# The down projection of a decoder block as seven Strassen products instead of one full product

## What the kernel must compute

```python
h = modulate(rms_norm(x, norm_ffn_g), sh2, sc2)          # 1024 x 1024
gu = silu(h @ w_gate) * (h @ w_up)                       # 1024 x 2816
x = x + g2 * (gu @ w_down)                               # w_down is 2816 x 1024
return rms_norm(x, final_norm_g)
```

## Time and profile before

| | |
|---|---|
| median of three runs | 1543.34 us (1543.19 to 1545.88) |
| the profiled execution, its own time | 1546.7 us |
| its span, first to last instruction | 1545.0 us |
| mean granted TensorE clock | 0.977 |
| PE busy | 1441.9 us, 93% of the span |
| DVE, ACT, POOL busy | 54%, 45%, 44% |
| gate and up products on PE | from 854 us to 1289.5 us |
| down products on PE | from 1289.5 us to 1537.9 us |

### The profile page before, as it was taken

One profiled execution on the slowest core, in us unless ns is written; L12 is line 12 of the kernel. 1 busy time (PEld: TensorE's weight loads), 2 busy tenths in 40 slices (PEclk: granted clock), 3 DMA queues, 4 the chain that ended last, 5 costly groups with the idle time before them and its releaser, 6 DMA issues.

```text
span 1545.0 us, 20466 instructions
## 1 busy us (share of the span) xinstructions
PE 1441.9 (93%) x7471; PEld 1225.5 (79%) x7471; DVE 831.4 (54%) x1479; ACT 694.1 (45%) x1334; POOL 676.0 (44%) x464
## 2 busy tenths in 40 slices
PE   1899899999999989899899899999999999899998
PEld 1887688887889978889688678888888887788886
DVE  5645879994644656654545763443333333615414
ACT  4524446631656655666633544333333331423321
POOL 2331222161110422062000898888888882642640
PEclk9999999999999998999799999999999999999999
DMA  9121122331203442210411032222222226653641
GB/s 372 46 82 57 66 83 81 133 129 62 77 29 124 138 163 88 92 62 21 151 55 42 31 106 82 83 82 82 82 82 82 82 96 229 215 156 138 204 135 55
DMA packets 106541, 161.27 MB, mean 104 GB/s; under 512 B 7021, under 2 KB 65573, under 8 KB 105418
## 3 DMA queue, kind: packets, MB, share of 16 engines
q1 hardware_dynamic: 106442, 159.97, 30.8%
HBM read 127.37 MB, written 32.58 MB: 104 GB/s over the span
## 4 chain that ended last, share of the span: by engine, by line
PE 82%; DVE 8%; issue 3%; ACT 3%; DMA 3%; POOL 1%; SPq 1%; DVEq 0%; ACTq 0%; POOLq 0%
PE PS L1775 21%; PE PS L1776 21%; PE PS L1777 21%; PE PS L1943 6%; PE PS L1913 5%; PE PS L1930 2%; PE PS L1931 2%; DMA rawb<-in_w_down_dram 1%; DVE LP L1504 1%; PE PS L1929 1%; DVE acc L1207 1%; PE PS L1975 1%; DVE marks_c L1344 1%; DMA adar<-in_ada_w_dram 1%; DVE sel L1311 1%
## 5 line engine op out<-in xcount | busy, mean ns | idle before, releaser
L839 POOL TENSOR_TENSOR BS<-rawb,BS 128x1024 fp32r<-128x1024 f32 x44 | 107.3, 2443 | 127.6 <-ACT BS L1123 127.6
L826 POOL TENSOR_TENSOR WS<-WSf,WS 128x512 fp32r<-128x512 f32 x110 | 162.7, 1487 | 0.7 <-ACT WS L1067 0.7
L1067 ACT CAST WS<-WSf 128x512 fp32r<-128x512 f32 x110 | 68.4, 622 | 202.1 <-POOL WSf L816 201.1
L816 POOL TENSOR_TENSOR WSf<-rawg 128x512 f32<-128x512 f32 x55 | 77.3, 1406 | 172.0 <-PE PS L1777 170.8
L1943 PE MATMUL PS<-Vn,PT 128*128 128x64 f32 x1152 | 145.4, 273 | 0.0
L1775 PE MATMUL PS<-BS,AS 128*128 128x512 f32 x352 | 137.9, 392 | 6.9 <-POOL BS L839 6.6
L1943 PEld LDWEIGHTS PS<-Vn,PT 128*128 128x128 f32 x1152 | 141.8, 195 | 0.0
L1775 PE MATMUL PS<-yh,WS 128*128 128x512 f32 x352 | 137.9, 392 | 2.9 <-DVE yl L1636 2.9
L1777 PE MATMUL PS<-yh,WS 128*128 128x512 f32 x352 | 137.7, 391 | 0.0
L1776 PE MATMUL PS<-yl,WS 128*128 128x512 f32 x352 | 137.5, 391 | 0.0
L1777 PE MATMUL PS<-BS,AS 128*128 128x512 f32 x352 | 137.4, 390 | 0.0
(11 more groups left out here) (300 smaller groups left out, 3530.7 us busy)
## 6 DMA issues: line engine op xcount, KB each, us to landing
rawb<-in_w_down_dram SPq DMA_DIRECT2D x44, 512.0 KB, 3.5
adar<-in_ada_w_dram SPq DMA_DIRECT2D x32, 512.0 KB, 3.8
raw<-in_w_in_dram SPq DMA_DIRECT2D x24, 512.0 KB, 3.9
qkv_scratch<-stage SPq DMA_DIRECT2D x48, 256.0 KB, 2.0
rawg<-in_w_gate_dram SPq DMA_DIRECT2D x22, 512.0 KB, 4.7
rawu<-in_w_up_dram SPq DMA_DIRECT2D x22, 512.0 KB, 4.3
gu_scratch<-Cu SPq DMA_DIRECT2D x44, 256.0 KB, 2.0
rawa<-gu_scratch SPq DMA_DIRECT2D x44, 256.0 KB, 3.5
```

The lines of the kernel that those rows point to most:

```text
L816: pool.tensor_tensor(WSf[m % N_SLOT][:], left(i, mat, a), left(i, mat, b), ALU.add if sign > 0 else ALU.subtract).then_inc(ws_sum, 1)
L826: pool.tensor_tensor(lo, WSf[m % N_SLOT][:] if b else left(i, mat, a), hi.bitcast(F32), ALU.subtract).then_inc(ws_ready, 1)
L839: pool.tensor_tensor(b[:, 1, :], rawb[m % 2][:], b[:, 0, :].bitcast(F32), ALU.subtract).then_inc(gb_lo, 1)
L1067: act.copy(WS[m % N_SLOT][:, 0], src).then_inc(ws_hi, 1)
```

## The change

The down projection becomes seven products of half matrices. gu is split into quadrants by odd and even hidden block and by token half, w_down by odd and even hidden block and by column half. For each of the seven forms, in the order of `DOWN`, 11 steps are run, one for each pair of hidden blocks, so 77 steps in place of 44. A step loads one 128x512 block of a gu quadrant or of a sum of two, and one or two 128x512 blocks of w_down, and runs 12 matmuls into four PSUM banks; consecutive products use the two halves of PSUM in turn.

- In the gate and up stage DVE forms five sums or differences of gu quadrants in each round (`gu_sum`) and SP stores them. With "22" and "11", which are stored as they are, seven blocks are stored in a round where there were four.
- In the down stage POOL forms the sum or difference of two w_down blocks for five of seven products (`down_sum`, 55 steps), and the `lo` part for the steps that are not in `DOWN_BY_V`. These 20 steps (four in each of those five products) get the `lo` part of the weights from DVE.
- `rawa` has three buffers, `rawb` four (each of two 128x512 parts). AS and BS keep six slots.
- Finished products are copied by ACT (form 1 into two quadrants, forms 5 and 4 into one) or added and subtracted by DVE (`down_evac`) in four held quadrants CD; the last use of a quadrant goes through g2 and the residual. They stand in DVE's program behind every second `down_low`.
- The eight residual loads are issued one by one, behind steps 11, 13, ... 25, g2 behind step 28 and the gain behind step 44. Step 4's loads stand with those of steps 0 to 3, ahead of the last stores.
- The last four tiles: GpSimd multiplies their left half by the gain ahead of time, ACT squares that half ahead of time and scales it at the end, DVE does the right half.

The diff, cut to its core:

```diff
+DOWN = ["1", "5", "3", "4", "2", "7", "6"]
+N_DOWN = len(DOWN) * PAIRS
+DOWN_SLOTS = 6
+DOWN_RAW_A = 3
+DOWN_RAW_B = 4
+GU_SUM = {"2": ("12", "22", 1), "7": ("21", "22", -1), "1": ("11", "22", 1), "5": ("11", "21", 1), "6": ("12", "11", -1)}
+RIGHT = {"1": ((0, 0), (1, 1), 1), "2": ((0, 0), None, 0), "3": ((0, 1), (1, 1), -1), "4": ((1, 0), (0, 0), -1),
+         "5": ((1, 1), None, 0), "6": ((0, 0), (0, 1), 1), "7": ((1, 0), (1, 1), 1)}
+DOWN_BY_V = [m for m in DOWN_SUMS if m % PAIRS % 3 == 1]
...
@@ SP
             def load_down(m):
+                form, j = DOWN[m // PAIRS], m % PAIRS
+                if m >= DOWN_RAW_A:
+                    sp.wait_ge(ga_lo, m - DOWN_RAW_A + 1)
...
+                sp.wait_ge(gu_out[form], GU_BASE[form] + 16 * (j + 1))
+                sp.dma_start(rawa[m % DOWN_RAW_A][:], gu_dram[int(form) - 1, j]).then_inc(ga_in[m % DOWN_RAW_A], 16)
+                if m >= DOWN_RAW_B:
+                    low_done(sp, m - DOWN_RAW_B)
+                elif m % 2 == 0:
+                    sp.wait_ge(ws_ready, AT_FF[PAIRS - 1, m // 2, FORMS[-1]] + 1)
+                for e, part in enumerate(RIGHT[form][0:2]):
+                    if part:
+                        row, col = (2 * j + part[0]) * P, part[1] * BANK
+                        sp.dma_start(rawb[m % DOWN_RAW_B][:, e, :],
+                                     w_down[row:row + P, col:col + BANK]).then_inc(gb_in[m % DOWN_RAW_B], 16)
...
+            for m in range(5, N_DOWN):
+                load_down(m)
+                if m == 7:
+                    store_sums(PAIRS - 1)
+                step, rest = divmod(m - PAIRS, 2)
+                if rest == 0 and 0 <= step < TT:
+                    sp.wait_ge(x_tile[step], 48)
+                    sp.dma_start(x1s[step // 4][:, step % 4, :], x1_dram[step * P:(step + 1) * P, :]).then_inc(x1_in, 16)
@@ POOL
+            for m in range(N_DOWN):
+                if m + 1 in DOWN_SUMS:
+                    down_sum(m + 1)
+                if m not in DOWN_BY_V:
+                    down_part(m)
@@ ACT
             def down_high(m):
+                before = m - DOWN_SLOTS
                 if m < 2:
                     act.wait_ge(x_lo, 3)
+                elif before < 0:
                     act.wait_ge(pr_pe, len(SEQ_FF))
+                elif before % PAIRS == PAIRS - 1:
+                    act.wait_ge(dn_pe, TT // 2 * (before // PAIRS + 1))
                 else:
+                    act.wait_ge(dj_pe, before - before // PAIRS + 1)
...
+                if m in DOWN_SUMS:
+                    act.wait_ge(gb_sum, DOWN_SUMS.index(m) + 1)
+                act.copy(BS[m % DOWN_SLOTS][:, 0, :], rawb[m % DOWN_RAW_B][:, 0, :]).then_inc(gb_hi, 1)
@@ DVE
             def down_low(m):
...
+                if m in DOWN_BY_V:
+                    b = BS[m % DOWN_SLOTS]
+                    dve.wait_ge(gb_hi, m + 1)
+                    dve.tensor_tensor(b[:, 1, :], rawb[m % DOWN_RAW_B][:, 0, :], b[:, 0, :].bitcast(F32),
+                                      ALU.subtract).then_inc(gb_lo_v, 1)
 
             for m, (i, mat, form) in enumerate(SEQ_FF):
                 combine(m)
+                if mat == 0 and i >= 1 and form in ("2", "4", "3"):
+                    gu_sum(i - 1, 2 + ("2", "4", "3").index(form))
...
                 if mat == 1 and form == "7":
                     gate_times_up(i, "22", 3, 7)
                     gate_times_up(i, "11", 4, 8)
+                    gu_sum(i, 0)
+                    gu_sum(i, 1)
...
+            def down_result(q, p, tt, held=True):
+                half, col = int(q[0]) - 1, int(q[1]) - 1
+                cols = slice(col * BANK, (col + 1) * BANK)
+                ps = PS[:, 4 * (p % 2) + tt, :]
+                if held:
+                    chained(dve.tensor_tensor(ps, ps, CD[q][:, tt, :], ALU.add))
+                chained(dve.tensor_tensor(ps, ps, g2r[:, cols], ALU.mult))
+                return dve.tensor_tensor(x1s[half][:, tt, cols], ps, x1s[half][:, tt, cols], ALU.add)
...
+                if form == "5":
+                    last = down_add("11", p, tt, ALU.subtract)
+                elif form == "3":
+                    chained(down_add("22", p, tt, ALU.add))
+                    last = down_result("12", p, tt)
+                elif form == "4":
+                    last = down_add("11", p, tt, ALU.add)
+                elif form == "2":
+                    chained(down_add("22", p, tt, ALU.subtract))
+                    chained(down_result("21", p, tt))
+                    ps = PS[:, 4 * (p % 2) + tt, :]
+                    chained(dve.tensor_tensor(ps, CD["22"][:, tt, :], g2r[:, BANK:D], ALU.mult))
+                    last = dve.tensor_tensor(x1s[1][:, tt, BANK:D], ps, x1s[1][:, tt, BANK:D], ALU.add)
+                elif form == "7":
+                    last = down_result("11", p, tt)
+                else:
+                    last = down_result("22", p, tt, held=False)
...
+            for m in range(2, N_DOWN + 2 * TT):
+                if m < N_DOWN:
+                    down_low(m)
+                if m < len(GU_ORDER):
+                    gu_sum(PAIRS - 1, m)
+                p, j = divmod(m - PAIRS - DOWN_SLOTS, PAIRS)
+                if p >= 1 and p < len(DOWN) - 1 and j % 2 == 0 and j < TT:
+                    down_evac(p, j // 2)
@@ PE
+            for p in range(len(DOWN)):
+                late = LATE_DOWN if p == len(DOWN) - 1 else 1
+                for j in range(PAIRS - late):
+                    m = p * PAIRS + j
                     pe.wait_ge(ga_lo, m + 1)
+                    low_done(pe, m)
                     for tt in range(TT // 2):
+                        if j == 0:
+                            bank_free(p, tt)
+                        last = down(m, tt, j == 0, False)
                     last.then_inc(dj_pe, 1)
```

More of the change, by code:

```diff
@@ L442, in build, with low_done @@
         gb_lo = sem("gb_lo")
-        x1_in = [sem(f"x1_in{i}") for i in range(2)]
-        g2_in = sem("g2_in")
+        x1_in = sem("x1_in")
+        def low_done(engine, m):
+            by_v = sum(e <= m for e in DOWN_BY_V)
+            if m + 1 - by_v:
+                engine.wait_ge(gb_lo, m + 1 - by_v)
+            if by_v:
+                engine.wait_ge(gb_lo_v, SEM_USED + by_v)
         dj_pe = sem("dj_pe")
@@ L639, in _ @@
                             load_ff(i + 1, mat, n)
+                    if mat == 0 and i >= 1:
+                        store_sums(i - 1)
                 if i == PAIRS - 1:
-                    load_down(0)
-                    load_down(1)
-                for e, q in enumerate(("21", "12", "22", "11")):
-                    n, half = int(q[0]) - 1, int(q[1]) - 1
-                    sp.wait_ge(mul_ok, 4 * i + e + 1)
-                    sp.dma_start(gu_dram[2 * i + n, :, half * BANK:(half + 1) * BANK], Cu[q][:]).then_inc(gu_out[q], 16)
@@ L647, in _ @@
[L647 to L661 removed]
+                    for m in range(5):
+                        load_down(m)
@@ L1100, in copies @@
                 else:
-                    for q in {"2": ("21", "22"), "4": ("11",), "3": ("12",)}[form]:
-                        act.wait_ge(gu_out[q], 16 * i)
+                    act.wait_ge(gs_ok, len(GU_ORDER) * i)
+                    if form in ("2", "4"):
+                        stored = "4" if form == "2" else "3"
+                        act.wait_ge(gu_out[stored], GU_BASE[stored] + 16 * i)
                 if form == "2":
@@ new lines, in down_evac @@
+            def down_evac(p, tt):
+                if p == 2 and tt == 0:
+                    dve.wait_ge(x1_in, 16 * TT)
+                    dve.wait_ge(g2_out, 32)
+                dve.wait_ge(dn_pe, TT // 2 * p + tt + 1)
+                if p in COPIED_OUT:
+                    first, step = COPIED_OUT[p]
+                    dve.wait_ge(cd_ok, first + step * tt)
+                form = DOWN[p]
+                if form == "5":
[15 more added lines that the diff above has]
+                    last = down_result("22", p, tt, held=False)
+                last.then_inc(dn_ev, 1)
@@ L2047, in _, with down @@
                 last.then_inc(pr_pe, 1)
-            def down(m, tt, nh, first, stop):
-                a, b = AS[m % 6], BS[m % 6]
-                rows, cols = slice(tt * P, (tt + 1) * P), slice(nh * BANK, (nh + 1) * BANK)
-                return three(PS[:, 2 * tt + nh, :], (a[:, 0, rows], a[:, 1, rows]), (b[:, 0, cols], b[:, 1, cols]), first, stop)
-            for g in range(2):
-                for j in range(FT - LATE_DOWN):
-                    m = g * FT + j
+            def down(m, tt, first, stop):
+                a, b = AS[m % DOWN_SLOTS], BS[m % DOWN_SLOTS]
+                rows = slice(tt * P, (tt + 1) * P)
+                return three(PS[:, 4 * (m // PAIRS % 2) + tt, :], (a[:, 0, rows], a[:, 1, rows]), (b[:, 0, :], b[:, 1, :]),
+                             first, stop)
@@ L2070, in _ @@
                     last.then_inc(dj_pe, 1)
-                pe.wait_ge(ga_lo, (g + 1) * FT)
```

(14 more changed lines are left out.)

252 lines of the change are left out of this document (147 added, 105 removed).

## The result

The changed kernel takes a median of 1531.26 us (20 runs, 1527.26 to 1545.07) beside 1545.98 us for the kernel before on the same chips (20 runs, 1542.54 to 1556.57). The ratio is 0.99, with a 95% interval of 0.9881 to 0.992. So it is faster, by 15 us, a little less than half of the 33 us forecast, and its time lies above the range of 1503 to 1523 us.

A forecast was written before the change was run, and what follows sets the result against it. PE was taken as the bound, in down by its number of matmuls. -29.9 - 8.7 - 0.4 + 2 + 2.5 + 1.5 = -33.0 us gave a median of 1510.3 us from 1543.3, range 1503 to 1523 us.

The forecast's parts named there:

- The matmuls: Down stage: 924 matmuls in place of 1056, all on the path, at 0.2269 us each, -29.9 us.
- The residual loads: Down stage: loads spread behind steps 11 to 25, 5.4 us apart; the old hole and its ramp go, -8.7 us.
- Gate and up: Five `gu_sum` a round fit beside POOL and DVE's other work, 0; 23 us as the other end.
- The price of a `lo` part beside POOL: A DVE operation with both inputs in SBUF takes 1.19 us beside a busy POOL, 0.69 alone.
- DVE's evacuations: Steps 61 to 76 of down: DVE's work about level with the time at hand; +2 us, of 0 to 8.
- rival B: Down: reloading weights through `rawb` sets the pace; mild 1513 to 1530 us, chance 0.09; slower than before, 0.03.
- The last tiles: After the last matmul: narrower square, left half's scaling on ACT, early work hidden under the last product's matmuls; -0.4 us.
- the start: First steps of down: less work made ahead, waits at steps 2, 5, 6 and 8; +2.5 us and +1.5 for a ramp.
- My sign for the forecast: POOL at over 85% busy in products 1, 3, 4, 7 and 6, stretches included, would show the forecast right.
- A: Products with sums: POOL and DVE set the pace, 8 to 15 us instead of 2; 1513 to 1524 us, chance 0.18.
- B's sign for itself: Down: POOL idle for rawb DMAs and landing above 4.5 us would point to weight reloading as the pace.
- C's size: Start of down costs as much as before, all 8.7 us back instead of 4; 1515 to 1518 us, chance 0.09.

The follow-up runs named there:

- the cut form 2: Changed kernel, three gu buffers, with five of the six DVE evacuation operations of each form 2 tile left out; 1518.61 us in one run.
- the one experiment on it: On six gu buffers, new product order and moved scalings: step 2's `lo` part ahead of the last gu sums, stores two steps later; median 1523.89 us.
- all rings together: Changed kernel with six gu buffers, six weight buffers and eight AS and BS slots; median 1517.86 us, ratio 0.9809 against the kernel before.

## Why the prediction was right in direction and wrong in size

**Right.** The matmuls: 924, -29.9 us, and at 0.2269 us a matmul between 1320 and 1470. The residual loads: issued from 1310.2 to 1346.3 us, 5.2 apart on average (7 intervals), landing in 5.8 us instead of 9.3, and no gap waits for them. Gate and up: 435 us as before, at 0. The price of a `lo` part beside POOL: from step 61 on 1.21 us (gu) and 1.28 (weights), where I took 1.2.

**Wrong, 1: "DVE's evacuations", +2, measured +11.8.** The working compared 49 us of work between `lo` part 61 and step 76 with 43.5 + 5.4 = 48.9 us of time. The work was right: 22 parts, 18.9 us for form 2 (4 x 4.7), 4.2 for form 7, 49.5 in all. What was wrong is the rest. The span from step 61's part (1448.4) to step 76's last (1503.0) is 54.6 us, so DVE also stood idle for some 5 us: that is the reload, which rival B had in POOL's ring of weight buffers, and which sits in the gu ring, one buffer smaller and ahead of the weights in SP's queue. And the time at hand was not 48.9 but 45.5 us. Step 61's slot comes free when PE is done with step 55, at 1447.5 us, and step 73, at which all of the last four steps are wanted, was due at 1493.9: that is 17 steps (46.3 us) where 48.9 us are 18, and the part began 0.9 us behind its slot. The 9.0 us lost at the start shift both ends of this and take nothing from it, as the reserve was full again; ACT's cast for step 61 had waited for PE:

```profile
1447.69 0.62 ACT L1189 CAST AS<-rawa 128x512 fp32r<-128x512 f32 x1 [0.63 <-PE PS L1933]
```

54.6 less 45.5 is 9.1 us late, and nearly all of the 2.6 that are left is the slower clock after the second hole (2.3). Shown by the six gu buffers (late loss 4.1) and by the cut form 2 (none).

**Wrong, 2: "The last tiles", -0.4, measured +4.2.** I let GpSimd's multiplications and the early squares "lie under the last product's matmuls (30 us)". They stand behind step 76's preparation on every engine, and that ended at 1503.0 us, with 13.3 us of matmuls left. I also left out that the kernel before scales its first four tiles at half time, and the changed one at the end. DVE from step 76's `lo` part to its last operation, as far as it is new:

```profile
1502.91 0.69 DVE L1864 TENSOR_TENSOR PS<-PS,CD 128x512 f32<-128x512 f32 x1
...
1507.04 1.19 DVE L1915 TENSOR_SCALAR stat<-stat 128x4 f32<-128x4 f32 x1
...
1513.43 1.28 DVE L1903 SCALAR_TENSOR_TENSOR x1s<-x1s,rstd,fgr 128x1024 f32<-128x1024 f32 x1
1514.63 0.69 DVE L1865 TENSOR_TENSOR PS<-PS,g2r 128x512 f32<-128x512 f32 x1
...
1523.08 0.75 DVE L1903 SCALAR_TENSOR_TENSOR x1s<-x1s,rstd,fgr 128x512 f32<-128x512 f32 x1
```

Two form 7 tiles to 1507.0, a small operation and four scalings to 1514.6, and only then the last product's four tiles, to 1523.8: 20.9 us of list against 13.3 us of matmuls. The first of those tiles was done on PE while DVE was still scaling; leaving the four scalings out gave 4 to 5 us.

**Wrong, 3: the start, +4.0, measured 9.0.** Step 2's hole came as worked out, 1.8 us where I had 1.1; DVE's two gu sums took a turn each beside POOL:

```profile
1287.63 1.76 POOL L889 TENSOR_TENSOR BS<-rawb,BS 128x512 fp32r<-128x512 f32 x1 [8.57 <-ACT BS L1193]
1289.36 1.73 POOL L882 TENSOR_TENSOR rawb<-rawb 128x512 f32<-128x512 f32 x1
1291.06 1.71 POOL L889 TENSOR_TENSOR BS<-rawb,BS 128x512 fp32r<-128x512 f32 x1
1298.68 1.29 POOL L882 TENSOR_TENSOR rawb<-rawb 128x512 f32<-128x512 f32 x1 [5.92 <-DMA rawb<-in_w_down_dram]
1301.80 1.31 POOL L882 TENSOR_TENSOR rawb<-rawb 128x512 f32<-128x512 f32 x1 [1.83 <-DMA rawb<-in_w_down_dram]
```

```profile
1288.15 3.49 DVE L1809 TENSOR_TENSOR GS<-Cu 128x512 f32<-128x512 f32 x2
1291.57 1.75 DVE L1814 TENSOR_TENSOR AS<-rawa,AS 128x512 fp32r<-128x512 f32 x1
```

But the holes at steps 5 and 8 were 2.8 and 2.3 us where I had 0.4 and "similar". SP issues step 5's loads from 1293.3 us on, behind that `lo` part, and POOL makes step 5's sum at 1298.7; then it wants step 6's sum first, waits 1.8 us for its weights (1301.80), and step 5's low part ends at 1304.3. Behind step 7 stand the five stores, and only then step 8's loads:

```profile
1293.34 0.32 SPq L660 DMA_DIRECT2D rawa<-gu_scratch  x1
...
1297.69 3.23 SPq L674 DMA_DIRECT2D gu_scratch<-GS  x5
1301.02 0.52 SPq L660 DMA_DIRECT2D rawa<-gu_scratch  x1
```

My working had POOL's order in it, but not its wait for step 6's weights, and it took step 8 as "similar" without counting the stores' 3.2 us in SP's queue. For steps 5 to 8 it also had the landing too small, at 3.5 us. Weight blocks issued from 1292.5 to 1303 us, and the stretch behind the hole of step 5, with the DMA engines' share (1.05) and GB/s last:

```profile
rawb<-in_w_down_dram SPq DMA_DIRECT2D x8, 256.0 KB, 6.2
```

```profile
1304.40:1312.00 7.60, 7.56 (x32) 6.04 (x33) 3.90 (x3) 1.49 (x3) 4.17 (x3) 1.00 1.05 401
```

They landed in 6.2 us in the median, and step 8's, issued until 1303.1, were there at 1310.3. With six gu buffers the start loses 3.3 to 4.4 us in the six executions with six slots and 2.4 to 4.0 in the four with eight, near my figure; without POOL's sums 0.8 (six gu buffers and eight slots) to 2.6 (three buffers). How the rest divides between the stores, the landing and POOL's order stays open: in the one experiment on it, the holes at steps 2 and 5 shrank, and one of 2.4 us came behind the stores' new place.

**The rivals.** A had the right mechanism in the wrong place. POOL was busy for 65.4 of 80 us (82%) from 1320 on, product 5, which has no sums, included, and PE had no hole there. My sign for the forecast, over 85% in all five products with sums, came in product 3 alone (26.0 of 29.9 us); product 4 had 25.3 of 30.0, product 7 21.3 of 32.0 and product 6, up to its last `lo` part, 22.5 of 29.0. What the sums cost, 18.5 us in all with three gu buffers, falls at the start (6.4) and late (11.9). Its price was too high: a pair of POOL and DVE operations takes 1.70 to 1.73 us (1287.63, 1289.36, 1291.06), which is the stretch of 0.46 of the earlier trace rows on POOL's pitch of 1.25, where A had added 0.60. (The Trainium skill, SBUF — State Buffer, § Who interferes with whom, calls the port pair that VectorE and GpSimd share an exclusive lock; the trace agrees within 0.15 us a pair, as the two pitches, 1.25 and 0.60, add to 1.85. The experiment without DVE's weights fits it, as the remaining operations became longer, but does not prove it.) B's sign for itself, POOL idle for weights, came, at a landing of 4.0 us over the whole stage, below B's 4.5, and of 6.2 us in the first ten us. C's size came, not its cause. The range left all these together out: I had taken them as alternatives, and they came in one kernel, one at the start and two behind 1470 us.

## What to carry to other kernels

When matmuls are taken out, ask of every engine not what it does in a step but what it does from the last point of full reserve to the last thing wanted, work and waits, and count the reserve once. In a queue that issues in order, look first at the smallest ring of buffers: here it held back the loads of the rings behind it, and three more buffers there were the cheapest gain of this study (six gu buffers, 10 us; all rings together, 1517.9 us). Work shifted from DVE to POOL, where both read two operands from SBUF, gained nothing that the profiles here could tell; leaving operations out did.

## What the runs showed of the hardware

- DVE and POOL operations with both inputs in SBUF take turns, at 1.70 to 1.73 us for one of each, in a long backlog on both: DVE's 0.69 becomes 1.75 and POOL's 1.28 becomes 1.73.
- Weight blocks of 256 KB landed in a median of 4.0 us over the whole stage, 4.2 from 1320 to 1400 us (DMA share 0.94, 323 GB/s) and 6.2 from 1292.5 to 1303 us, behind which the share was 1.05 at 401 GB/s; before, 512 KB landed in 3.5 us at 177 GB/s.
- After a hole of 4.8 us TensorE started matmuls 0.43 us apart, its lower level (granted clock 0.50). In all, the holes of the changed kernel add to 14.5 us and the time lost in down to 20.5 us, so that the ramps cost 6.0 us, but not evenly: 0.1 and 0.3 us behind the holes of 1.8 and 2.8 us at 1293 and 1304 us, and 1.6, 1.8 and 2.3 us behind those of 2.3, 2.8 and 4.8 us at 1315, 1479 and 1503 us. Of two holes of 2.8 us one was followed by the lower level and one was not.
